# Heads' steps of a bidirectional mLSTM: exponent weights, keys and values in high and low parts

## The reference, cut to what matters

```python
def step(carry, xs):                       # one chunk of 128 tokens
    C, n, m = carry
    qc, kc, vc, li, lf = xs
    b = jnp.cumsum(lf, axis=-1)
    d = b[..., :, None] - b[..., None, :] + li[..., None, :]
    d = jnp.where(lower, d, -jnp.inf)
    m_inter = b + m[..., None]
    m_t = jnp.maximum(m_inter, jnp.max(d, axis=-1))
    w_inter = jnp.exp(m_inter - m_t)
    a = jnp.einsum('bhtd,bhsd->bhts', qc, kc) * jnp.exp(d - m_t[..., None])
    num = w_inter[..., None] * jnp.einsum('bhtd,bhde->bhte', qc, C) + jnp.einsum('bhts,bhse->bhte', a, vc)
    den = w_inter * jnp.einsum('bhtd,bhd->bht', qc, n) + jnp.sum(a, axis=-1)
    h = num / jnp.maximum(jnp.abs(den), jnp.exp(-m_t))[..., None]
    ...
    wk = jnp.exp(g - m_new[..., None])[..., None] * kc
    C_new = decay[..., None, None] * C + jnp.einsum('bhsd,bhse->bhde', wk, vc)
    n_new = decay[..., None] * n + jnp.sum(wk, axis=-2)
    return (C_new, n_new, m_new), h
...
h = jax.nn.sigmoid(heads(mo)) * (h_fwd + h_bwd)
h = h * lax.rsqrt(jnp.mean(h * h, axis=-1, keepdims=True) + EPS)
```

## Time and profile before

| | |
|---|---|
| median of three runs | 2406.71 us (2405.79 to 2408.76) |
| profiled execution, its own time | 2404.15 us |
| span of the profiled execution | 2402.2 us |
| granted TensorE clock over the span | 0.998 |
| TensorE matmul busy | 2358.3 us (98%), 13524 instructions |
| VectorE busy | 1452.8 us (60%) |
| ScalarE busy | 905.2 us (38%) |
| GpSimd busy | 1225.5 us (51%) |

### The profile page before, as it was taken

The page is one execution under the profiler, slowest core; times in us unless marked ns, Lnnn a source line. Parts: engine busy times, 40 slices in busy tenths (PEclk is TensorE's granted clock), DMA queues, the critical chain, the costliest instruction groups (busy, mean ns, idle before and its releaser), DMA issues.

```text
span 2402.2 us, 36382 instructions
## 1 busy us (share of the span) xinstructions
PE 2358.3 (98%) x13524; PEld 2123.4 (88%) x13524; DVE 1452.8 (60%) x2556; ACT 905.2 (38%) x1854; POOL 1225.5 (51%) x1496
## 2 busy tenths in 40 slices
PE   7999999999999999999999999999999999999998
PEld 5888888888888888888888889999999999989886
DVE  6623367334672347634686642999878787965537
ACT  5212443224442244423544112554333334542443
POOL 3154520455204552066462548797555555976576
PEclk9999999999999999999999999999999999999999
DMA  3122211321112311123455443332444434477873
GB/s 138 51 103 93 62 42 27 108 84 62 36 38 97 99 45 42 45 99 115 131 161 168 133 158 115 117 126 88 151 146 133 159 128 147 139 269 263 280 240 119
DMA packets 186952, 285.61 MB, mean 119 GB/s; under 512 B 14344, under 2 KB 126824, under 8 KB 186776
## 3 DMA queue, kind: packets, MB, share of 16 engines
q1 hardware_dynamic: 139320, 241.99, 30.4%
q10 hardware_dynamic: 47456, 41.31, 5.9%
HBM read 203.48 MB, written 79.68 MB: 118 GB/s over the span
## 4 chain that ended last, share of the span: by engine, by line
PE 84%; DVE 7%; DVEq 2%; DMA 2%; POOL 1%; ACT 1%; issue 1%; SPq 0%; ACTq 0%; POOLq 0%
PE ps L3220 18%; PE ps L3222 18%; PE ps L3221 18%; PE ps L3721 3%; PE ps L3722 3%; PE ps L3723 3%; PE ps L3266 3%; PE ps L3268 3%; PE ps L3267 3%; PE ps L3446 2%; PE ps L3356 2%; PE ps L3371 2%; PE ps L3466 2%; PE ps L3348 1%; PE ps L3479 1%
## 5 line engine op out<-in xcount | busy, mean ns | idle before, releaser
L3220 PE MATMUL ps<-ht_h,unit_h 128*128 128x512 f32 (+1 forms) x1408 | 508.3, 361 | 0.3 <-issue 0.3
L3222 PE MATMUL ps<-ht_h,unit_l 128*128 128x512 f32 (+1 forms) x1408 | 498.3, 354 | 0.0
L3221 PE MATMUL ps<-ht_l,unit_h 128*128 128x512 f32 (+1 forms) x1408 | 498.2, 354 | 0.0
L1361 POOL TENSOR_TENSOR unit_h<-unit_raw,colt 128x256 fp32r<-128x256 f32 x320 | 203.5, 666 | 352.9 <-DMA unit_raw<-w 352.5
L3222 PEld LDWEIGHTS ps<-ht_h,unit_l 128*128 128x128 f32 x1408 | 266.0, 189 | 37.3
L3220 PEld LDWEIGHTS ps<-ht_h,unit_h 128*128 128x128 f32 x1408 | 266.3, 189 | 36.6 <-issue 0.7
L3221 PEld LDWEIGHTS ps<-ht_l,unit_h 128*128 128x128 f32 x1408 | 266.4, 189 | 35.8 <-issue 0.5
L1365 POOL TENSOR_TENSOR unit_l<-unit_raw,unit_h 128x256 fp32r<-128x256 f32 x320 | 245.5, 799 | 11.7 <-issue 0.4
L3220 PE MATMUL ps<-operands,unit_h 128*128 128x320 f32 (+1 forms) x740 | 230.5, 311 | 1.8 <-POOL sum_l L1531 1.0
L3222 PE MATMUL ps<-operands,unit_l 128*128 128x320 f32 (+1 forms) x740 | 229.3, 310 | 0.0
L3221 PE MATMUL ps<-operands,unit_h 128*128 128x320 f32 (+1 forms) x740 | 229.3, 310 | 0.0
(11 more groups left out here) (376 smaller groups left out, 5770.0 us busy)
## 6 DMA issues: line engine op xcount, KB each, us to landing
unit_raw<-w SPq DMA_DIRECT2D x149, 512.0 KB, 3.9
bw<-exponent_rows_scratch ACTq DMA_DIRECT2D x40, 256.0 KB, 3.7
down_raw<-wdn SPq DMA_DIRECT2D x24, 384.0 KB, 4.9
side_raw<-side_sum_scratch SPq DMA_DIRECT2D x24, 384.0 KB, 6.1
block_raw<-weight_sum_scratch SPq DMA_DIRECT2D x16, 576.0 KB, 4.3
gate_scratch<-g_st SPq DMA_DIRECT2D x28, 256.0 KB, 3.5
stage<-f_scratch SPq DMA_DIRECT2D x28, 256.0 KB, 3.1
side_sum_scratch<-stage SPq DMA_DIRECT2D x14, 512.0 KB, 2.8
```

Of the source, the lines that this page charges most:

```text
L1361: nc.gpsimd.tensor_tensor(unit_h[:, slot, k:k + 2], unit_raw[:, slot, k:k + 2], one_col.unsqueeze(2).to_broadcast([P, 2, P]), ALU.mult)
L3220: mm(out_ap, wh, hi(k + k_first), start=first and k == 0, stop=False, skip_group_check=skip)
L3221: mm(out_ap, wh, lo(k + k_first), start=False, stop=False, skip_group_check=skip)
L3222: ins = mm(out_ap, wl, hi(k + k_first), start=False, stop=last and k == kts - 1, skip_group_check=skip)
```

## The change

It does four things.

1. The three products with `v_tok` (line 3348 and both directions of line 3371) become three fp32r matmuls each, `values_product`: high with the values' high part and two ones columns (258 columns), high with the values' low part (256), low with the values' high part (258). The queries' products with the state stay as they are.
2. VectorE makes the parts of `ex` in three instructions with a drain where there was one, and a low part of the scaled keys, `keys_low`, once for each update. `keys_low(0, i + 1)` stands before `gated(i)` and `state(1, i)`, `keys_low(1, i + 1)` behind them; each waits for GpSimd's `scale_keys` (`m_wk`), and `m_update` on TensorE waits for it (`m_wl`).
3. GpSimd makes the parts of the values, `split_values`: for each of ten blocks it waits for VectorE's `evac_vo`, writes the high part, drains, writes the low part in place. It stands ahead of `mlstm(h)` in GpSimd's stream, and so ahead of `take` of A0. `m_numden(0)` waits for all ten (`m_vs`).
4. The scratch for software transfers is 2 KB. Two pairs of semaphores become one (`p_row` takes the counts of `p_tc` and `c_pad`), which changes no order.

The diff, without the hunks that only rename semaphores and widen a memset:

```diff
--- before.py
+++ after.py
@@ -479,7 +479,9 @@
 
     mq_t = at("mq_t", 122880, [P, 2, T])
     mk_t = at("mk_t", 133120, [P, 2, T])
-    v_tok = at("v_tok", 143360, [P, NB, DH + 1])
+    v_raw = at("v_raw", 143360, [P, NB, DH])
+    v_l = at("v_low", 143360, [P, NB, DH], F32R)
+    v_h = at("v_high", 212864, [P, NB, DH + 2], F32R)
     h_acc = at("h_acc", 153664, [P, NB, DH])
     c_st = at("c_st", 163904, [P, 2, 2, DH + 1])
 
...
@@ -504,8 +506,11 @@
     bias_vo = at("bias_vo", 194240, [P, 2 * DH])
 
     ex = [at("ex_0", 196288, [P, 2, P]), at("ex_1", 187488, [P, 2, P])]
+    ex_l = [at("ex_low_0", 196288, [P, 2, P], F32R), at("ex_low_1", 187488, [P, 2, P], F32R)]
+    ex_h = at("ex_high", 223200, [P, 2, P], F32R)
     qw = at("qw", 197312, [P, 2, 2, P])
-    wk = at("wk", 199392, [P, 2, DH])
+    wk_h = at("wk_high", 199392, [P, 2, DH], F32R)
+    wk_l = at("wk_low", 224224, [P, 2, DH], F32R)
 
     v_hl = [at("v_hl_a", 196288, [P, 6, 2, HD], F32R), at("v_hl_b", 207584, [P, NB - 6, 2, HD], F32R)]
 
...
@@ -635,14 +640,13 @@
     s_gs = [sem("gate_stored0"), sem("gate_stored1")]
     s_gd = [sem(f"late_gate_stored{k}") for k in range(3)]
 
-    p_row = sem("rows_zeroed_abs_args")
+    p_row = sem("row_steps_and_pads_by_vector")
     p_in = sem("rows_split")
     p_act = sem("softplus_and_rows80_exp")
     p_out = sem("rows_stored")
     p_80 = sem("rows80_landed")
     p_w = sem("inter_rows_stored")
     p_col = sem("cols_transposed")
-    p_tc = sem("tokcol_ready")
 
     m_sel = sem("m_head_columns")
     a_sel = sem("a_next_head_columns")
...
@@ -654,6 +658,8 @@
     m_a = sem("m_weights")
     m_q = sem("m_query_scaled")
     m_wk = [sem("m_wk_fwd"), sem("m_wk_bwd")]
+    m_wl = sem("m_wk_low")
+    m_vs = sem("m_values_split")
     m_nd = sem("m_numden")
     m_h = sem("m_numden_read")
     m_cu = [sem("m_update_fwd"), sem("m_update_bwd")]
...
@@ -1427,7 +1432,7 @@
                 if i and updates_to(d, i - 1):
                     pool.wait_ge(m_cu[d], 8 * h + updates_to(d, i - 1))
                 c = chunk_of(d, i)
-                nc.gpsimd.tensor_tensor(wk[:, d].rearrange("p (e t) -> p e t", e=2), mk_t[:, :, c * P:(c + 1) * P],
+                nc.gpsimd.tensor_tensor(wk_h[:, d].rearrange("p (e t) -> p e t", e=2), mk_t[:, :, c * P:(c + 1) * P],
                                         tcol(3, d, h, c).unsqueeze(2).to_broadcast([P, 2, P]), ALU.mult
                                         ).then_inc(m_wk[d], 1)
 
...
@@ -1454,10 +1459,21 @@
                 if h == HEADS - 1:
                     take(lambda k: a_unit(k, A_UNITS - 1), h)
 
+            def split_values(h):
+
+                for blk in range(NB):
+                    pool.wait_ge(ev_dve, GROUPS[("M", h, 12 + blk)][3])
+                    nc.gpsimd.tensor_tensor(v_h[:, blk, 0:DH], v_raw[:, blk], one_col.to_broadcast([P, DH]), ALU.mult)
+                    pool.drain()
+                    nc.gpsimd.tensor_tensor(v_l[:, blk], v_raw[:, blk], v_h[:, blk, 0:DH].bitcast(F32), ALU.subtract
+                                            ).then_inc(m_vs, 1)
+
+            split_values(0)
             for h in range(HEADS - 1):
                 mlstm(h)
                 for u in range(M_UNITS):
                     take(lambda k, u=u: m_unit(k + 1, u), h)
+                split_values(h + 1)
             mlstm(HEADS - 1)
 
             def take_b(p):
...
@@ -2416,7 +2432,7 @@
                 elif shift:
                     dve.wait_ge(s_os[blk % 2], lin(lambda k: 16 * 5 * (k + shift), h))
                 bank = GROUPS[("M", h + shift, 12 + blk)][1]
-                V.tensor_tensor(v_tok[:, blk, 0:DH], ps[:, bank, 0:DH], bias_vo[:, 0:DH], ALU.add)
+                V.tensor_tensor(v_raw[:, blk], ps[:, bank, 0:DH], bias_vo[:, 0:DH], ALU.add)
                 V.tensor_tensor(o_st[:, blk % 2], ps[:, bank, DH:2 * DH], bias_vo[:, DH:2 * DH],
                                 ALU.add).then_inc(ev_dve, 1)
 
...
@@ -2508,7 +2524,20 @@
                     dve.wait_ge(m_ev, lin(lambda k: NB // 2 * k + i + 1, h))
                 dve.wait_ge(m_x, lin(lambda k: NB * k + i + 1, h))
                 kept = s_sv[:, min(i, NB - 1 - i)]
-                V.tensor_tensor(ex[i % 2][:], ex[i % 2][:], kept, ALU.mult).then_inc(m_a, 1)
+                V.tensor_tensor(ex_h[:], ex[i % 2][:], kept, ALU.mult)
+                V.tensor_tensor(ex[i % 2][:], ex[i % 2][:], kept, ALU.mult)
+                dve.drain()
+                V.tensor_tensor(ex_l[i % 2][:], ex[i % 2][:], ex_h[:].bitcast(F32), ALU.subtract).then_inc(m_a, 1)
+
+            def keys_low(d, i, h):
+
+                if not updates(d, i):
+                    return
+                dve.wait_ge(m_wk[d], 8 * h + updates_to(d, i))
+                c = chunk_of(d, i)
+                V.scalar_tensor_tensor(wk_l[:, d].rearrange("p (e t) -> p e t", e=2), mk_t[:, :, c * P:(c + 1) * P],
+                                       tcol(3, d, h, c), wk_h[:, d].rearrange("p (e t) -> p e t", e=2).bitcast(F32),
+                                       ALU.mult, ALU.subtract).then_inc(m_wl, 1)
 
             def state(d, i, h):
 
...
@@ -2570,14 +2599,19 @@
                 if dense:
                     next_columns(h + 1)
                 weights(0, h)
+                for d in range(2):
+                    keys_low(d, 0, h)
                 for i in range(NB):
                     normalise_h(i, h)
                     state(0, i, h)
                     if i + 1 < NB:
                         weights(i + 1, h)
+                        keys_low(0, i + 1, h)
                     if i >= 5:
                         gated(i, h)
                     state(1, i, h)
+                    if i + 1 < NB:
+                        keys_low(1, i + 1, h)
 
             def scores_max(j, h):
 
...
@@ -3338,22 +3372,29 @@
                         ins = mm(ps[:, 2, P * n:P * n + P], mk_t[:, dt, t], mq_t[:, dt, t], start=dt == 0, stop=dt == 1)
                 ins.then_inc(m_sc, 1)
 
+            def values_product(out, hi, lo, c, last):
+
+                mm(out[:, 0:DH + 2], hi, v_h[:, c], start=True, stop=False, skip_group_check=True)
+                mm(out[:, 0:DH], hi, v_l[:, c], start=False, stop=False, skip_group_check=True)
+                return mm(out[:, 0:DH + 2], lo, v_h[:, c], start=False, stop=last, skip_group_check=True)
+
             def m_numden(i, h):
                 if i == 0:
-                    pe.wait_ge(ev_dve, lin(lambda k: GROUPS[("M", k, 21)][3], h))
+                    pe.wait_ge(m_vs, NB * h + NB)
                 else:
                     pe.wait_ge(m_h, lin(lambda k: NB * k + i, h))
                 pe.wait_ge(m_a, lin(lambda k: NB * k + i + 1, h))
                 for d in range(2):
-                    ins = mm(ps[:, 3 + d, 0:DH + 1], ex[i % 2][:, side(d, i)], v_tok[:, chunk_of(d, i)],
-                             start=True, stop=fresh(d, i))
+                    ins = values_product(ps[:, 3 + d], ex_h[:, side(d, i)], ex_l[i % 2][:, side(d, i)], chunk_of(d, i),
+                                         fresh(d, i))
                 if i:
                     pe.wait_ge(m_q, lin(lambda k: 9 * k + i, h))
                 for d in range(2):
                     if not fresh(d, i):
                         pe.wait_ge(m_c[d], lin(lambda k: 8 * k + updates_to(d, i - 1), h))
                         for dt in range(2):
-                            ins = mm(ps[:, 3 + d, 0:DH + 1], qw[:, d, dt], c_st[:, d, dt], start=False, stop=dt == 1)
+                            ins = mm(ps[:, 3 + d, 0:DH + 1], qw[:, d, dt], c_st[:, d, dt], start=False, stop=dt == 1,
+                                     skip_group_check=True)
                 ins.then_inc(m_nd, 1)
 
             def m_update(d, i, h):
...
@@ -3367,9 +3408,10 @@
                     pe.wait_ge(m_c[1 - d], lin(lambda k: 8 * k + before, h))
                 if updates_to(d, i) > 1:
                     pe.wait_ge(m_c[d], lin(lambda k: 8 * k + updates_to(d, i) - 1, h))
+                pe.wait_ge(m_wl, 16 * h + updates_to(0, i) + (updates_to(1, i) if d else updates_to(1, i - 1)))
                 for dt in range(2):
-                    ins = mm(ps[:, 5 + dt, 0:DH + 1], wk[:, d, dt * P:(dt + 1) * P], v_tok[:, chunk_of(d, i)],
-                             start=True, stop=True)
+                    t = slice(dt * P, (dt + 1) * P)
+                    ins = values_product(ps[:, 5 + dt], wk_h[:, d, t], wk_l[:, d, t], chunk_of(d, i), True)
                 ins.then_inc(m_cu[d], 1)
 
             def m_turn(i, h):
...
@@ -3923,7 +3965,7 @@
         "bvo": np.ascontiguousarray(np.concatenate([bv, bo], axis=1)),
         "sink": np.ascontiguousarray(snk),
     }
-    nc = bacc.Bacc("TRN2", target_bir_lowering=False, num_devices=1)
+    nc = bacc.Bacc("TRN2", target_bir_lowering=False, num_devices=1, dynamic_dma_scratch_size=2048)
     args = [nc.dram_tensor(n, v.shape, mybir.dt.from_np(v.dtype), kind="ExternalInput").ap()
             for n, v in arrays.items()]
```

(9 more changed lines are left out.)

2 lines of the change are left out of this document (removed).

## The result

The change makes the kernel slower, by about as much as forecast. After: 2428.97 us, the median of four runs (2427.48 to 2431.52), beside 2406.74 us for the kernel before (2405.79 to 2408.76, four runs). The ratio is 1.0092, with an interval of 1.0075 to 1.0110: +22.2 us, where +18.7 (2425 us) was forecast. The profiled execution took 2428.16 us, with a span of 2426.0 us and a mean granted clock of 0.993; that span is 23.8 us above the one before.

A forecast was written before the change was run, and what follows sets the result against it. TensorE, busy 98% of the span, was taken to bound the kernel. Terms -15.6 + 23.3 + 6.0 + 5.0 = +18.7 us on the 2406.7 us median gave 2425 us, range 2413 to 2438.

The forecast's parts named there:

- The likeliest case: The forecast itself, 2425 us for the whole kernel, slower than before by 18.7 us; given 65%.
- The products, -15.6: TensorE's 208 products with values cost 0.36 instead of 0.435 us each, saving 15.6 us; bounds 14.6 to 16.6.
- The waits at the heads' beginnings, +23.3: TensorE waits for GpSimd's take of A0 behind the splitting: 6.5 us in head 0, 5.6 in each other; bounds 22 to 25.
- The clock behind them, +6.0: After each of the four waits for A0, matmuls run at half clock, costing 1.5 us each; bounds 0 to 12.
- The rival with a clock that holds: The clock stays at full through the waits at the heads' beginnings, giving 2419 us; chance 14%.
- Heads 0 to 2, VectorE's added work at 0: In these heads' steps VectorE's idle time hides its added instructions: 0 us, bounds 0 to 4.
- The rival with VectorE late in every head (+15): Heads 0 to 2 each lose what head 3 does, 15 us more, giving 2440 us; chance 13%.
- Head 3, +5.0: VectorE's added work delays TensorE in head 3's steps 5, 7 and 8, about 5 us together; bounds 2 to 12.
- Step 5: Head 3: `keys_low` waits for GpSimd's keys, backward state 1.1 us later; 1.6 us with the step's lost gain.
- step 7: Head 3: `keys_low` and `gated(6)` follow GpSimd's late keys, so TensorE waits 0.4 to 2.5 us for the state; 1.1 taken.
- step 8: Head 3: `m_turn(7)`'s 1.38 us wait for ScalarE grows by 2.0 us through VectorE's added instructions in that chain.
- Scratch, 0: The scratch for software transfers costs nothing, as hardware transfer queues carry the load: 0 us.

The follow-up runs named there:

- e6_no_lows: e1 without VectorE's low parts of `ex` and keys, high parts standing in for them in the third pass; 2394.10 us, ratio 0.9949.
- e1: The changed kernel with GpSimd's take of A0 moved ahead of the splitting of the values; 2397.07 us, ratio 0.9963 to the kernel before.
- e2: The kernel before plus only GpSimd's splitting of the values, into a tile nobody reads, and the small scratch; 2438.10 us, ratio 1.0131.
- e3_filler: The changed kernel with 40 filler matmuls (48 in head 0) on TensorE ahead of A0; 2421.23 us, ratio 1.0063 to the kernel before.
- e4_scratch: The kernel before with only the 2 KB scratch for software transfers; 2405.92 us, ratio 1.0000.

## Why the prediction was right

The forecast was 2425 us, range 2413 to 2438; measured 2428.97. The likeliest case came true, with its mechanism, and the sum was 3.5 us low by the medians (5.2 by the two profiles, which the steps below add up to). By its steps:

- **The products, -15.6.** Right as a price: 0.075 us each, shown by e6_no_lows in three heads (3.9 us for 52 products). In head 3 it was lost again, which is counted there.
- **The waits at the heads' beginnings, +23.3.** 22.0 by the view of waits, 22.4 by the marks, inside the bounds of 22 to 25. Shown twice: they vanish when the take is moved (e1), and come alone with the splitting (e2). No second wait followed, as said.
- **The clock behind them, +6.0.** Right in kind and too small: some 7 us by e3_filler, 8.7 by the marks. The one wait that the earlier trace rows offered was followed by 3.4 us at half clock, and I took that length for all. The stretches after the new, longer waits were 5.5, 6.4, 3.3 and 5.1 us. The bound of 12 covered it. The rival with a clock that holds is refuted.
- **Heads 0 to 2, VectorE's added work at 0.** It cost 0.4 + 0.5 + 0.5 = 1.4 us, most of it ahead of `m_numden(3)`, inside the bound of 4. I looked at step 4 and not at the place where only one short group stands between the scores and the next `m_numden`. The rival with VectorE late in every head (+15) is refuted.
- **Head 3, +5.0.** Gross +5.9: 1.95 net and the 3.9 us that the products should save. Step 5 was forecast at 1.1 us for the late state and has 0.95; step 7 at 1.1 and has 0.71; step 8 went from 1.38 to 2.07 and not 2.0 more. The shortfall there is made up by waits for `ex_low` and `qw` in step 5, `ex_low` ahead of step 8 and `c_st` in step 2, which I had not listed. That this sum came so near with its parts partly wrong is luck. And VectorE's added work, to which I charged all of it, is only part of the cause: in e6_no_lows, without that work, head 3 also lost 3.7 of its 3.9 us, to longer waits for `qw` and `h_acc` and a half-clock stretch.
- **Attention, not in the sum.** +1.8 us between the profiles. I can't put this on the change: e4_scratch, in the order of before, has +1.0 us in the same stretches, with more such waits. The kernels with the splitting have +1.0 to +2.8 us there, so a part of the change in it is not ruled out either. That the profile before had few of these waits may be why the spans differ by 23.8 us and the medians by 22.2.
- **Scratch, 0.** Right (e4_scratch).

What stays open is what starts a half-clock stretch behind short waits, and what ends one sooner or later. The third, of 3.3 us, came behind a wait as long as that ahead of the second, of 6.4 us. Nor was the cause of the attention's small waits tested.

## What to carry to other kernels

Where a change adds work to a helper engine, look at what already stands behind it in that engine's order before adding up busy time: here eighty instructions of splitting cost little where nothing urgent stood behind them, and their place ahead of one take cost 22 us of waits and 7 to 9 of clock. Move what an urgent consumer needs ahead of the new work, and move new waits behind results that don't need them; these two edits turned +22 us into -12.8, the first of them most of it. A gain on the bounding engine counts only in the stretches where it bounds: three heads gave 0.075 us a product, the fourth next to nothing.
